# Sixteen projection blocks of a second layer as eight pairs of seven block products, with the shift taken from PSUM and the values centred in their turn

## The chip, the cores and the metric

The kernel runs on one core of one Trainium2 chip. Its time is the device time of the execution in microseconds; the time of a kernel is the median of its runs. Before the change the median of 3 runs is 2240.72 us (2239.9 to 2247.26).

## What is computed

A two-layer model over 1024 tokens of width 1024, in float32. The first layer (a state-space mixer, stick-breaking attention and a feed-forward block) isn't touched. The second is a hybrid layer: one projection `u = h @ w_in` of the normalised input feeds a gated linear attention (GLA) of 4 heads and an RWKV-7 recurrence of 8 heads. Cut to what matters here:

```python
h = _rmsnorm(x, norm_w)
u = (h @ w_in).astype(f32)
gla_u, rwkv_u = u[..., :GLA_IN], u[..., GLA_IN:]
gq, gk, gv, glr, gg = _split(gla_u, GLA_SPLITS)
log_a = jax.nn.log_sigmoid(glr @ gla_gate_up + gla_gate_bias) / GLA_TAU
o = _gla_chunked(q, k, v, log_a)              # chunks of 64 tokens
gla_out = rms(o) * gla_norm_w * jax.nn.silu(gg)
prev = jnp.pad(shifted_cols, ((0, 0), (1, 0), (0, 0)))[:, :-1]
mixed = shifted_cols + (prev - shifted_cols) * rwkv_mu
r, rk, rv, wl, al = _split(mixed, RWKV_SHIFT_SPLITS)
y = _rwkv7_scan(r_h, decay, k_h, v_h, kk, a)  # y linear in v
mu = jnp.mean(y, axis=-1, keepdims=True)
var = jnp.mean(jnp.square(y - mu), axis=-1, keepdims=True)
y = (y - mu) * lax.rsqrt(var + RWKV_GN_EPS) * rwkv_ln_w + rwkv_ln_b
rwkv_out = (y + bonus) * jax.nn.silu(rg)
return x + jnp.concatenate([gla_out, rwkv_out], axis=-1) @ w_out
```

## The kernel before

Five engines have a queue of instructions each, written out by hand in one block per phase; they meet at semaphores. The change lies in two phases.

**`second_in_phase`** (L2847) computes the projection in 30 blocks of 128 output columns: block 0 (the two low-rank parts), 1 to 12 (keys, receptances and values of four RWKV head pairs), 13 (narrow: the GLA gate's 16 columns), 14 to 25 (GLA queries, keys, values and gates) and 26 to 29 (RWKV gates). A block's weights are 128 partitions x 1024 float32, two raw buffers deep. SP loads them; POOL scales them by `WSCALE` (L2981); ACT makes the float16 high part (L3215); POOL subtracts it for the low part (L2987); PE multiplies high x high, high x low and low x high over 8 slices of the contraction and 2 halves of the tokens, 48 matmuls of 512 columns (`product`, L3022 to L3024); ACT empties PSUM (L3235). The input's own parts lie in `second_x_hi` and `second_x_lo` (`S.xhi`, `S.xlo`).

Around the blocks each engine works through the rest, one piece per block. DVE mixes each of blocks 0 to 12 with its shift by one token (L3330 to L3332: a difference, then a multiply-add), makes keys (L3347), receptances (L3358) and values (L3371 to L3382), and then, in this order with solving steps between, the GLA gate (L3430 to L3443), its query and key factors (L3452 on) and the GLA units. POOL computes `keys` (L2995) for each head pair. The solving steps (`substitute`, L3410 to L3424) invert a triangular system for all chunks at once, loaded by SP as one transfer (L2963) of what was parked in DRAM; step n needs step n - 1. The eight GLA units of 128 tokens (0 to 7) start at block 22: PE's turns (L3110), scores (L3116), states (L3124), outputs (L3133 to L3136) and sums (L3151) lie before (`amid`) and after (`behind`) the products, and use DVE's `unit_front` (L3460), `unit_squares` (L3468) and `unit_state` (L3476) and ACT's `unit_out` (L3271) and `unit_sums_out` (L3276). All of a unit waits for the state of the unit before it.

The first layer's `ffn_up_phase` (L2076 on) already multiplies pairs of blocks by seven block products. There SP loads (L2160), POOL forms the sums of the weights (L2197 to L2202), DVE makes the low parts (of the weights L2459, of the next input L2474) and ACT the high parts (of that input L2363). `LAST_USE` (L2073) names the product that reads a part last.

**`rwkv_units_phase`** (L3490) runs the recurrence in eight units of 128 tokens. Per unit PE transposes the parked vectors (`turned`, L3673), makes the maps (L3692 to L3712) and `recur`, then `means` (L3773) and `variances` (L3777) of the unit before; ACT copies the removal factors (L4001), key-values (L4005) and y (L4021) out of PSUM, squares (L3981) and takes roots (L3986, L3988); DVE subtracts the mean (`deviation`, L3879), forms `result` (L3887 to L3893) and `gated` (L3897, L3899). The order of each queue is the order of its loop over c, from -1 to 7. ACT's and DVE's loops before open as:

```python
for c in range(-1, NUNIT):                      # ACT
    if c >= 2:
        high(c - 2)
    if 2 <= c < 2 + GLA_HEADS:
        act.wait_ge(s_gv, 2 * (c - 1))
        nc.scalar.activation(mhi[:, c - 2, :], ...)
    if ahead:
        act.wait_ge(s_akm, n + 1)
        nc.scalar.activation(aa[...], aa_ps, ACT.Copy)   # L4001
```

The output products (L3820 to L3822) end the kernel.

## Time and profile before

| | before |
|---|---|
| median of 3 runs | 2240.72 us |
| runs | 2239.9, 2240.72, 2247.26 us |
| the profiled execution | 2238.72 us |
| its span, first to last instruction | 2237.0 us |
| mean granted clock of TensorE | 0.989 |
| PE busy | 2140.8 us (96%) |
| PE's weight loads (PEld) | 1435.5 us (64%) |
| DVE busy | 1573.6 us (70%) |
| ACT busy | 1001.5 us (45%) |
| POOL busy | 616.3 us (28%) |

The profile is one execution. Busy time is that of instructions which do work; waiting at a semaphore and issuing a DMA don't count. The clock is the share of full speed that TensorE was granted. A "releaser" is what ended an idle time, inferred from the semaphores. PE is matrix work, DVE VectorE, ACT ScalarE, POOL GpSimd, and SPq the queue of the engine that issues the loads. Names are those of buffers in the program: `wraw_z`, `whi_z`, `wlo_z` are the raw weights and their two parts, `ps` is PSUM, and the working arrays (`second_work`, `ffn_out`, `z`, `down_squares`) carry different things in different phases.

### The profile page before, as it was taken

How to read it: one execution, taken by the hardware profiler on the slowest of the kernel's cores; microseconds unless marked ns; L12 is line 12 of the kernel's file. 1: busy time of each engine (PE TensorE's matmuls, PEld its weight loads, DVE VectorE, ACT ScalarE, POOL GpSimd, SP SyncE). 2: the span in 40 equal slices, each digit the busy share in tenths (PEclk: the TensorE clock that was granted, in tenths of full speed). 3: DMA queues.
4: the chain of work that ended last, by engine and by line, in shares of the span. 5: the costliest groups of instructions: out<-in, count | busy, mean ns of one | idle time of the engine just before them, and what ended most of it. 6: DMA issues, size and time to landing. Idle time of an engine off the chain costs nothing. (4 is left out here: it accounts for less than half of the span.)

```text
span 2237.0 us, 45699 instructions
## 1 busy us (share of the span) xinstructions
PE 2140.8 (96%) x19060; PEld 1435.5 (64%) x19060; DVE 1573.6 (70%) x2081; ACT 1001.5 (45%) x1772; POOL 616.3 (28%) x399
## 2 busy tenths in 40 slices
PE   7999999999999899899999999999999999989998
PEld 4666665656666566568888885458644445578757
DVE  6966888988888655887888884256687675246654
ACT  3227775666666443544444443245554332124321
POOL 4456763200001220043333321000155432101160
PEclk9999999999999999999999999999999999999999
DMA  3113213677777622211111115326333622033422
GB/s 138 48 41 112 84 59 88 128 145 145 142 142 142 142 99 73 100 57 53 58 58 58 58 44 189 100 77 215 122 109 108 179 95 86 10 99 100 169 62 76
DMA packets 292086, 224.25 MB, mean 100 GB/s; under 512 B 205537, under 2 KB 255905, under 8 KB 290481
## 3 DMA queue, kind: packets, MB, share of 16 engines
q1 hardware_dynamic: 291888, 221.44, 36.1%
q8 instruction: 146, 2.39, 0.4%
q14 instruction: 52, 0.42, 0.1%
HBM read 148.46 MB, written 28.86 MB: 79 GB/s over the span
## 5 line engine op out<-in xcount | busy, mean ns | idle before, releaser
L1543 DVE TENSOR_TENSOR_SCAN att_left<-att_left,att_unseen_prefix 16x16 f32<-16x16 f32 (+5 forms) x144 | 183.3, 1274 | 34.2 <-ACT att_left L1382 34.2
L3022 PE MATMUL ps<-second_x_hi,whi_z 128*128 128x512 f16 (+1 forms) x480 | 178.8, 372 | 3.4 <-POOL wlo_z L2987 1.9
L1276 PE MATMUL ps<-x_hi,whi_z 128*128 128x348 f16 x560 | 176.0, 314 | 3.4 <-DVE att_q L1487 3.4
L3024 PE MATMUL ps<-second_x_hi,wlo_z 128*128 128x512 f16 (+1 forms) x480 | 178.5, 372 | 0.0
L3023 PE MATMUL ps<-second_x_lo,whi_z 128*128 128x512 f16 (+1 forms) x480 | 178.5, 372 | 0.0
L1278 PE MATMUL ps<-x_hi,wlo_z 128*128 128x348 f16 x560 | 174.9, 312 | 0.0
L1277 PE MATMUL ps<-x_lo,whi_z 128*128 128x348 f16 x560 | 174.8, 312 | 0.0
L2987 POOL TENSOR_TENSOR wlo_z<-wraw_z,whi_z 128x1024 f16<-128x1024 f32 x28 | 65.7, 2348 | 177.9 <-ACT whi_z L3215 177.9
L1502 DVE SCALAR_TENSOR_TENSOR att_left_split<-att_left,att_left_split 128x256 f16<-128x256 f32 (+7 forms) x128 | 106.9, 835 | 7.2 <-ACT att_left_split L1396 7.2
L1396 ACT ACTIVATE att_left_split<-att_left 128x256 f16<-128x256 f32 (+7 forms) x128 | 86.7, 679 | 38.1 <-DMA att_left_turned<-att_left_split 28.6
L1382 ACT ACTIVATE att_left<-ps 16x16 f32<-16x16 f32 (+5 forms) x144 | 86.1, 598 | 37.7 <-PE ps L1292 37.4
L3215 ACT ACTIVATE whi_z<-wraw_z 128x1024 f16<-128x1024 f32 x28 | 29.6, 1056 | 132.4 <-PE ps L3024 117.3
L1323 PE MATMUL ps<-att_left_turned,att_v_tokens 128*64 128x128 f16 x1728 | 63.3, 226 | 25.6 <-DMA att_left_turned<-att_left_split 18.3
L3022 PEld LDWEIGHTS ps<-second_x_hi,whi_z 128*128 128x128 f16 x480 | 46.9, 98 | 62.4 <-issue 6.3
L1234 POOL CAST att_v_meta_split<-att_v_meta 32x128 f16<-32x128 f32 x8 | 9.5, 1183 | 275.4 <-ACT att_v_meta L1388 275.4
L1276 PEld LDWEIGHTS ps<-x_hi,whi_z 128*128 128x128 f16 x560 | 54.7, 98 | 42.2 <-issue 14.7
L1323 PEld LDWEIGHTS ps<-att_left_turned,att_v_tokens 128*64 128x64 f16 x1728 | 53.2, 114 | 44.2 <-issue 34.8
L3023 PEld LDWEIGHTS ps<-second_x_lo,whi_z 128*128 128x128 f16 x480 | 47.0, 98 | 53.5 <-issue 3.6
L3024 PEld LDWEIGHTS ps<-second_x_hi,wlo_z 128*128 128x128 f16 x480 | 46.9, 98 | 53.3
L219 PE MATMUL ps<-x_hi,whi_xbc 128*128 128x348 f16 x240 | 75.6, 315 | 4.6 <-DVE x_lo L529 4.6
L2246 PE MATMUL ps<-x_hi,whi_z 128*128 128x257 f16 (+1 forms) x288 | 78.5, 273 | 0.0
L2247 PE MATMUL ps<-x_lo,whi_z 128*128 128x257 f16 (+1 forms) x288 | 78.4, 272 | 0.0
(694 smaller groups left out, 6675.6 us busy)
## 6 DMA issues: line engine op xcount, KB each, us to landing
wraw_z<-in_w_second SPq DMA_DIRECT2D x30, 512.0 KB, 3.7
wraw_z<-in_w_up SPq DMA_DIRECT2D x26, 512.0 KB, 3.6
wraw_z<-in_w_qkv SPq DMA_DIRECT2D x24, 512.0 KB, 4.7
wraw_z<-in_w_down SPq DMA_DIRECT2D x20, 512.0 KB, 3.8
raw_down<-in_w_down SPq DMA_DIRECT2D x20, 512.0 KB, 4.1
seg<-dt_a_sums SPq DMA_DIRECT2D x18, 512.0 KB, 5.0
...
```

The costliest lines, as they stand in the source:

```text
L1276: nc.tensor.matmul(lin_ps(g), hi, xhi, start=(kb == 0), stop=False)
L1277: nc.tensor.matmul(lin_ps(g), hi, xlo, start=False, stop=False)
L1278: last = nc.tensor.matmul(lin_ps(g), lo, xhi, start=False, stop=(kb == DB - 1))
L1323: nc.tensor.matmul(o_ps(n)[half(a)], vt[:, t.p % 2, (NSTEP - 1) * (x + 1) - t.j + m, half(a)], turned[t.slot][:, keys_at(t, a) + y * t.j + ...
L1382: nc.scalar.activation(of_head(t, a, 0, t.wide), z_ps(a)[0:t.rows, 0:t.wide], ACT.Sigmoid, scale=-0.125).then_inc(s_keep, 1)
L1396: last = nc.scalar.activation(left_part(e, 0, P * t.j), of_head(t, a, 0, P * t.j), ACT.Copy, scale=PSCALE)
L1502: last = nc.vector.scalar_tensor_tensor(low_, of_head(t, a, 0, P * t.j), PSCALE, high, ALU.mult, ALU.subtract)
L1543: nc.vector.tensor_tensor_scan(x, x, unseen, 1.0, ALU.mult, ALU.max).then_inc(s_scan, 1)
L2246: nc.tensor.matmul(out, hi, xhi, start=first and j == 0, stop=False, skip_group_check=True)
L3022: nc.tensor.matmul(out, hi, xhi, start=(j == 0), stop=False)
L3023: nc.tensor.matmul(out, hi, xlo, start=False, stop=False)
L3024: return nc.tensor.matmul(out, lo, xhi, start=False, stop=(j == DB - 1))
```

## The change

1. Blocks 14 to 29 are computed as 8 pairs. A pair's weights are the 2 x 2 blocks A11, A12 (first block, two halves of the contraction), A21, A22, and four sums S1 = A21 + A22, S2 = S1 - A11, S3 = A11 - A21, S4 = A12 - S2; the input has four sums of quarters likewise (`t16`). Seven products (P1 to P7) of 12 matmuls of 512 columns each take the place of 96. They stand on PE in the order P1, P4 of the pair before, P2, P6, P5, P7, P3. Two halves are added up inside PSUM; ACT copies P1, U2 (P1 + P6) and P5 out (`keep`), and DVE adds three of the four results (`quarter`) from PSUM.
2. POOL scales nothing any more and makes no low parts: the scale is folded into ACT's high part and DVE's low part. POOL forms the sums of the weights (`combine`), in which S1 and S2 lie in a buffer of their own and S3 and S4 in place of A11.
3. The sums and parts of the input are made in the first 12 blocks (`t_sums`, `t_lows` on DVE, `t_highs` on ACT).
4. The mix reads the shifted block from PSUM: ACT empties with a scale per column, and DVE adds in one operation. Both scales are small tables made at the start.
5. Gate, keys, solving steps and GLA units stand at new places in the pairs (`SOLVED_AT`; `gate_keys` in pair 3 ahead of A22's low part). SP's waits for A11, U (A21 and A22) and A12 are new.
6. In the RWKV units the values are turned by a product with `center` (identity less the mean of 64) in place of the transpose, so that y comes out centred. `means` and `deviation` go, `variances` take the place of `means`, DVE's `gated` moves to ahead of `keys`, and ACT's `high` and the gated part move behind the copies of the removal.

The diff, cut to its core, with the common indentation left out:

```diff
+SEVEN0 = GLA0 + 1
+SEVENS = (SECOND_B - SEVEN0) // 2
+ORDER_2 = ("P1", "P2", "P6", "P5", "P7", "P3", "P4")
+SPLITS_2 = ("A11", "A12", "S2", "S1", "S3", "S4", "A22")
+FIRST_GATED = (GLA0 + GG - SEVEN0) // 2
+FIRST_G = (G0 - SEVEN0) // 2
+T2_ROUNDS = DB // 2
+SOLVED_AT = {2: (1, 8), 3: (8, 14), 4: (14, 20), 5: (20, 26), "first gate": (26, HALF - 1)}
...
+        t16 = [ctx.enter_context(nc.sbuf_tensor(n, [P, 4, DB // 2, BANK], F16)) for n in ("t2_hi", "t2_lo")]
+        kept = ctx.enter_context(nc.sbuf_tensor("seven_kept", [P, 3, BANK], F32))
+        mu_prev, mu_now = (kept[:, 2, a * 16:a * 16 + GLA0] for a in range(2))
...
-    for i in range(SLOTS, SECOND_B):
...
+    for i in range(SEVENS):
+        g, u = L.w[SEVEN0 + 2 * i], L.w[SEVEN0 + 2 * i + 1]
+        if i == 0:
+            sp.wait_ge(L.cut, SEVEN0 - 1)
+        else:
+            sp.wait_ge(s_slo, split_low(i - 1, "S3"))
+        sp.dma_start(s32["A11"], half(g, 0)).then_inc(s_in["A11"], 16)
+        if i == 0:
+            sp.dma_start(s32["A12"], half(g, 1)).then_inc(s_in["A12"], 16)
+            sp.wait_ge(L.cut, SEVEN0)
+        else:
+            sp.wait_ge(s_comb, combined(i - 1, 4))
+            sp.wait_ge(s_slo, split_low(i - 1, "A22"))
+        sp.dma_start(L.raw[:, 1, :], u).then_inc(s_in["U"], 16)
+        if i:
+            sp.dma_start(s32["A12"], half(g, 1)).then_inc(s_in["A12"], 16)
+        if i < 2:
+            park(2 + i)
+            park_a(2 + i)
+        if i == 1:
             sp.wait_ge(s_asb, RWKV_P * 4 * 16)
             sp.wait_ge(s_parked[RWKV_P - 1], PARKS * 16)
+            sp.wait_ge(s_solve, 1)
...
-    def scaled(i):
-        if i < SECOND_B:
-            pool.wait_ge(L.landed[i % SLOTS], 16 * (i // SLOTS + 1))
-            raw = L.raw[:, i % SLOTS, :]
-            nc.gpsimd.tensor_scalar(raw, raw, WSCALE, 1.0, ALU.mult, ALU.mult).then_inc(s_w64, 1)
-
-    def low_part(i):
...
-            nc.gpsimd.tensor_tensor(L.lo[:, w, :], L.raw[:, w, :], L.hi[:, w, :], ALU.subtract).then_inc(L.cut, 1)
...
+    def combine(i):
+        pool.wait_ge(s_in["U"], in_(i, "U"))
+        pool.wait_ge(s_in["A11"], in_(i, "A11"))
+        if i:
+            pool.wait_ge(s_slo, split_low(i - 1, "S1"))
+        else:
+            pool.wait_ge(C.added, DB)
+        nc.gpsimd.tensor_tensor(s32["S1"], s32["A21"], s32["A22"], ALU.add).then_inc(s_comb, 1)
+        pool.wait_ge(s_comb, combined(i, 1))
+        nc.gpsimd.tensor_tensor(s32["S2"], s32["S1"], s32["A11"], ALU.subtract).then_inc(s_comb, 1)
+        pool.wait_ge(s_comb, combined(i, 2))
+        pool.wait_ge(s_slo, split_low(i, "A11"))
+        nc.gpsimd.tensor_tensor(s32["S3"], s32["A11"], s32["A21"], ALU.subtract).then_inc(s_comb, 1)
+        pool.wait_ge(s_in["A12"], in_(i, "A12"))
+        pool.wait_ge(s_slo, split_low(i, "A12"))
+        nc.gpsimd.tensor_tensor(s32["S4"], s32["A12"], s32["S2"], ALU.subtract).then_inc(s_comb, 1)
+
+    for b in range(RWKV_P - 1):
+        keys(b)
+    combine(0)
+    keys(RWKV_P - 1)
+    pool.wait_ge(s_tlo, t_split(T2_ROUNDS - 1))
+    nc.gpsimd.memset(flat[:, SUB * SUB:2 * SUB * SUB], 0.0).then_inc(s_solve, 1)
+    for i in range(1, SEVENS):
+        combine(i)
...
+    def block_product(i, name, out, of, start, end):
+        pe.wait_ge(s_slo, split_low(i, name))
+        for j in range(DB // 2):
+            hi, lo = (part16(i, name, part)[:, j * P:(j + 1) * P] for part in range(2))
+            xhi, xlo = of(j)
+            nc.tensor.matmul(out, hi, xhi, start=start and j == 0, stop=False, skip_group_check=True)
+            nc.tensor.matmul(out, hi, xlo, start=False, stop=False, skip_group_check=True)
+            last = nc.tensor.matmul(out, lo, xhi, start=False, stop=end and j == DB // 2 - 1, skip_group_check=True)
+        last.then_inc(s_p, 1)
...
+    def seven(i):
+        j = SEVEN0 + 2 * i
+        if i == 0:
+            pe.wait_ge(s_mixed, GLA0 - 1)
+        elif i >= 2:
+            pe.wait_ge(s_c21, nth_c21(i - 2))
+        block_product(i, "A11", bank_a(i), x_of(0, 0), True, False)
+        if i:
+            behind(j - 1)
+            fourth(i - 1)
+        pe.wait_ge(s_quarter, nth_quarter(i - 1, "C11") if i else GLA0)
+        block_product(i, "A12", bank_b, x_of(0, DB // 2), True, True)
+        amid(j)
+        if i == 0:
+            pe.wait_ge(s_tlo, t_split(T2_ROUNDS - 1))
+        pe.wait_ge(s_kept, nth_kept(i, "P1"))
+        block_product(i, "S2", bank_a(i), t_of(2), False, False)
+        if i == 0:
+            removal(RWKV_P - 1)
+        if i:
+            pe.wait_ge(s_quarter, nth_quarter(i - 1, "C12"))
+        block_product(i, "S1", bank_c, t_of(1), True, False)
+        behind(j)
+        pe.wait_ge(s_kept, nth_kept(i, "U2"))
+        block_product(i, "S3", bank_a(i), t_of(3), False, False)
+        if i == 0:
+            gate_products()
+        if i < SEVENS - 1:
+            amid(j + 1)
+        pe.wait_ge(s_kept, nth_kept(i, "P5"))
+        block_product(i, "S4", bank_c, x_of(1, DB // 2), False, True)
...
+    for i in range(SEVENS):
+        seven(i)
+    amid(SECOND_B - 1)
+    fourth(SEVENS - 1)
+    behind(SECOND_B - 1)
+    amid(SECOND_B)
+    behind(SECOND_B)
...
+    empty(GLA0)
+    for name in SPLITS_2[2:]:
+        part_high(0, name)
+    for i in range(SEVENS):
+        c = 2 * i - (UNIT0 - SEVEN0)
+        if i:
+            part_high(i, "S4")
+        act.wait_ge(s_p, made(i, "P1"))
+        if i:
+            act.wait_ge(s_quarter, nth_quarter(i - 1, "C11"))
+        keep(p1, bank_a(i))
+        if i:
+            if there(c - 2):
+                unit_sums_out(c - 2)
+            if i - 1 == FIRST_GATED:
+                nc.scalar.preload_act_table(ACT.Silu)
+            fourth_out(i - 1)
+            part_high(i, "A22")
+        part_high(i + 1, "A11")
+        if i - 1 >= FIRST_GATED:
+            gated(i - 1)
+        if i == 1:
             act.wait_ge(s_gv, 2)
             nc.scalar.activation(low, low, ACT.Exp).then_inc(s_exps, 1)
             act.wait_ge(s_exps, 1)
             nc.scalar.activation(low, low, ACT.Ln, bias=1.0).then_inc(s_ga, 1)
-        if j == GLA0 + 5:
+        if i == 2:
             act.wait_ge(s_gv, 5)
             nc.scalar.activation(low, gb, ACT.Exp).then_inc(s_ga, 1)
             nc.scalar.activation(gx, gb, ACT.Exp, scale=-1.0).then_inc(s_ga, 1)
-        if j == GLA0 + 6:
+        if there(c - 1):
+            unit_out(c - 1)
+        part_high(i + 1, "A12")
+        act.wait_ge(s_p, made(i, "P6"))
+        if i:
+            act.wait_ge(s_quarter, nth_quarter(i - 1, "C12"))
+        keep(u2, bank_a(i))
+        part_high(i + 1, "S2")
+        act.wait_ge(s_p, made(i, "P5"))
+        if i:
+            act.wait_ge(s_quarter, nth_quarter(i - 1, "C22"))
+        keep(p5, bank_c)
+        if there(c - 1):
+            unit_sums_out(c - 1)
+        part_high(i + 1, "S1")
+        if i == 2:
             act.wait_ge(s_gv, 7)
             nc.scalar.activation(low, low, ACT.Exp).then_inc(s_ga, 1)
+        part_high(i + 1, "S3")
         if there(c):
-            unit_sums_out(c)
+            unit_out(c)
...
-        nc.vector.tensor_scalar(d[:, 0:1], ub_[:, 0:1], -1.0, None, ALU.mult)
-        step(nc.vector.tensor_tensor(d[:, 1:SEQ], ub_[:, 0:SEQ - 1], ub_[:, 1:SEQ], ALU.subtract))
-        nc.vector.scalar_tensor_tensor(ub_, d, mu, ub_, ALU.mult, ALU.add).then_inc(s_mixed, 1)
+        nc.vector.scalar_tensor_tensor(now, before, mu_prev[:, mu_at(i):mu_at(i) + 1], now, ALU.mult, ALU.add).then_inc(s_mixed, 1)
...
+    for name in SPLITS_2[2:4]:
+        part_low(0, name)
+    for i in range(SEVENS):
+        c = 2 * i - (UNIT0 - SEVEN0)
+        if i:
+            part_low(i, "S4")
+            if there(c - 1):
+                unit_state(c - 1)
+            if i == 3:
+                gate_keys()
+            part_low(i, "A22")
+            part_low(i + 1, "A11")
+        if i == FIRST_G:
+            substitute(*SOLVED_AT["first gate"])
+        dve.wait_ge(s_p, made(i, "P2"))
+        dve.wait_ge(s_kept, nth_kept(i, "P1"))
+        if i < 2:
+            dve.wait_ge(s_parked[2 + i], PARKS * 16)
+        quarter(c11(i), bank_b, p1)
+        if i == 0:
+            for name in SPLITS_2[4:]:
+                part_low(0, name)
+            part_low(i + 1, "A11")
+            removal_out(RWKV_P - 1)
+        if i == 1:
+            gate_logs()
+            gate_sums(0)
+        if i == 2:
+            gate_query()
         if there(c):
             unit_front(c)
+        part_low(i + 1, "A12")
         if there(c - 1):
             unit_squares(c - 1)
-        if c in rest:
-            substitute(*rest[c])
+        part_low(i + 1, "S2")
         if there(c):
             unit_state(c)
+        dve.wait_ge(s_p, made(i, "P7"))
+        dve.wait_ge(s_kept, nth_kept(i, "P5"))
+        quarter(c22(i), bank_a(i), p5)
+        if i == 0:
+            gate_inputs()
+        if i == 1:
+            gate(gate_sums(1))
+        part_low(i + 1, "S1")
+        if there(c + 1):
+            unit_front(c + 1)
+        dve.wait_ge(s_p, made(i, "P3"))
+        dve.wait_ge(s_kept, nth_kept(i, "U2"))
+        quarter(c12(i), bank_c, u2)
+        if there(c):
+            unit_squares(c)
+        part_low(i + 1, "S3")
+        if i in SOLVED_AT:
+            substitute(*SOLVED_AT[i])
...
+    def turned_centered(c, b, kind):
+        for p in range(RWKV_P):
+            last = nc.tensor.matmul(bank(b)[:, p * P:(p + 1) * P], held(c)[:, kind, p, :], center[:, :], start=True, stop=True)
+        return last
...
-    def means(c):
-        pe.wait_ge(s_y, c + 1)
-        pe.wait_ge(s_rrc, min(c + 2, NUNIT))
-        nc.tensor.matmul(rr_ps, S.same[:, :], y[:, c % 2, :, :].rearrange("p q n -> p (q n)"), start=True, stop=True).then_inc(s_mean, 1)
-
     def variances(c):
         pe.wait_ge(s_sq, c + 1)
+        pe.wait_ge(s_rrc, min(c + 2, NUNIT))
...
-            means(c - 1)
+            variances(c - 1)
...
-        if c >= 1:
-            variances(c - 1)
...
-    def deviation(c):
-        dve.wait_ge(s_mean, c + 1)
-        yc = y[:, c % 2, :, :]
-        nc.vector.scalar_tensor_tensor(yc, rr_ps.rearrange("p (q n) -> p q n", q=RWKV_P), -1.0 / HD, yc, ALU.mult, ALU.add).then_inc(s_dev, 1)
...
+    nc.vector.scalar_tensor_tensor(center[:, :], S.same[:, :], -1.0 / HD, S.ident[:, :], ALU.mult, ALU.add).then_inc(s_center, 1)
...
-        if c >= 1:
-            deviation(c - 1)
+        if 2 <= c < 2 + GLA_HEADS:
+            gated(c - 2)
...
-        if 1 <= c <= GLA_HEADS:
-            gated(c - 1)
...
-        if c >= 2:
-            high(c - 2)
-        if 2 <= c < 2 + GLA_HEADS:
-            act.wait_ge(s_gv, 2 * (c - 1))
-            nc.scalar.activation(mhi[:, c - 2, :], o[:, c - 2, :], ACT.Copy).then_inc(s_ghi, 1)
...
+        if c >= 2:
+            high(c - 2)
...
+        if 2 <= c < 2 + GLA_HEADS:
+            act.wait_ge(s_gv, 2 * (c - 1))
+            nc.scalar.activation(mhi[:, c - 2, :], o[:, c - 2, :], ACT.Copy).then_inc(s_ghi, 1)
```

## Rows read from the trace of the kernel before

**Rows 1.** Windows: stretch, us, busy (count) of PE, PEld, DVE, ACT, POOL, PEclk, DMA.

```profile
1612.00:1758.60 146.60, 143.79 (x845) 64.92 (x843) 118.55 (x84) 68.75 (x67) 81.19 (x36) 1.00 0.39 119
1758.60:1974.20 215.60, 210.75 (x1420) 106.58 (x1416) 103.74 (x142) 50.74 (x54) 59.39 (x32) 1.00 0.25 80
```

**Rows 2.** PE's waits from 1758.6, then from 1974.2: total us, times, longest.

```profile
PE ps L3151 <- DVE down_squares L3468: 1.4, 1, 1.4
...
PE ps L3133 <- ACT ffn_out L3276: 0.8, 1, 0.8
...
PE ps L3673 <- ACT ru_removal L4001: 4.2, 5, 1.6
```

**Rows 3.** Windows, columns as in rows 1, two slices running.

```profile
1813.00:1831.00 18.00, 18.00 (x85) 8.21 (x84) 17.22 (x23) 9.23 (x7) 7.42 (x4) 1.00 0.10 36
1831.00:1849.10 18.10, 18.10 (x86) 8.16 (x85) 17.32 (x19) 2.41 (x3) 6.73 (x4) 1.00 0.18 58
```

**Rows 4.** Timeline of PE: start, us, engine, line, operation, out<-in, [idle before, releaser].

```profile
1954.93 0.38 PE L3022 MATMUL ps<-second_x_hi,whi_z 128*128 128x512 f16 x1
...
1957.95 0.38 PE L3024 MATMUL ps<-second_x_hi,wlo_z 128*128 128x512 f16 x1
```

**Rows 5.** Timelines of DVE, POOL and SP's queue, a pair of the first layer.

```profile
1084.13 1.74 DVE L2474 TENSOR_TENSOR second_x_lo<-gate_conv,second_x_hi 128x512 f16<-128x512 f32 x1 [0.22 <-ACT second_x_hi L2363]
...
1089.78 0.67 DVE L2459 SCALAR_TENSOR_TENSOR s_lo<-down_squares,s_hi 128x512 f16<-128x512 f32 x1
1090.38 0.68 DVE L2459 SCALAR_TENSOR_TENSOR s_lo<-wraw_z,s_hi 128x512 f16<-128x512 f32 x1
...
1084.05 1.27 POOL L2202 TENSOR_TENSOR wraw_z<-wraw_z 128x512 f32<-128x512 f32 x1 [2.76 <-DVE wlo_z L2459]
...
1092.60 0.33 SPq L2160 DMA_DIRECT2D wraw_z<-in_w_up  x1
...
1096.27 1.27 POOL L2197 TENSOR_TENSOR down_squares<-wraw_z 128x512 f32<-128x512 f32 x1 [7.29 <-DMA wraw_z<-in_w_up]
```

**Rows 6.** DVE's timeline through solving, gate and keys.

```profile
1812.67 1.88 DVE L3410 TENSOR_SCALAR z<-z 128x2048 f32<-128x2048 f32 x1
...
1818.46 2.29 DVE L3443 SCALAR_TENSOR_TENSOR second_work<-second_work,ffn_out 128x2048 f32<-128x2048 f32 x1
...
1825.99 0.47 DVE L3415 TENSOR_TENSOR second_work<-z 128x300 f32<-128x300 f32 x1
...
1839.81 0.70 DVE L3452 MEMSET ffn_out<- 128x768 f32 x1 [0.23 <-DVE z L3418]
...
1846.80 0.66 DVE L3415 TENSOR_TENSOR second_work<-z 128x480 f32<-128x480 f32 x1
```

**Rows 7.** Timelines of PE, DVE and POOL around the last values and keys.

```profile
1754.15 1.88 PE L3085 MATMUL ps<-ffn_out,same_chunk 128*128 128x512 f32 x4
...
1760.87 1.22 DVE L3372 TENSOR_TENSOR second_work<-second_work,ffn_out 128x1024 f32<-128x1024 f32 x1
...
1764.44 2.35 POOL L2995 TENSOR_TENSOR z<-second_work,ffn_out 128x1024 f32<-128x1024 f32 x1 [4.77 <-DVE second_work L3375]
```

**Rows 8.** SP's timeline; DMA issues: name, count, KB each, median us to landing.

```profile
1790.54 0.33 SPq L2963 DMA_DIRECT2D z<-removals  x1
...
z<-removals SPq DMA_DIRECT2D x1, 2048.0 KB, 7.7
```

**Rows 9.** PE's timeline in the first layer, and a window as in rows 1.

```profile
50.65 0.47 PE L219 MATMUL ps<-x_hi,whi_xbc 128*128 128x348 f16 x1 [3.58 <-DVE x_lo L529]
...
54.00:56.00 2.00, 2.00 (x8) 1.06 (x7) 1.97 (x3) 0.00 (x0) 0.00 (x0) 0.50 0.00 0
```

**Rows 10.** PE's timeline in one RWKV unit: means, transposes, products.

```profile
2057.08 1.12 PE L3773 MATMUL ps<-wraw_z,same_chunk 128*128 128x512 f32 x2
2058.04 1.04 PE L3673 MATMUL ps<-ident,second_work 128*128 128x128 f32 x8
...
2045.25 2.05 PE L3712 MATMUL ps<-down_squares,ffn_out 128*128 128x128 f32 x16
```

More of the change, by code:

```diff
@@ new lines, in second_in_phase @@
+        s32 = {"A11": half(L.raw[:, 0, :], 0), "A12": half(L.raw[:, 0, :], 1), "A21": half(L.raw[:, 1, :], 0), "A22": half(L.raw[:, 1, :], 1),
+               "S1": half(both, 0), "S2": half(both, 1), "S3": half(L.raw[:, 0, :], 0), "S4": half(L.raw[:, 0, :], 1)}
+        w16 = [{"A11": half(w[:, 0, :], 0), "A12": half(w[:, 0, :], 1), "A22": half(w[:, 1, :], 1),
+                "S1": x[:, 0, BANK:], "S2": x[:, 1, BANK:], "S3": x[:, 2, BANK:], "S4": x[:, 3, BANK:]} for w, x in ((L.hi, S.xhi), (L.lo, S.xlo))]
@@ L2892, in second_in_phase @@
+        first16 = {name: [half(kept[:, n, :].bitcast(F16), part) for part in range(2)] for n, name in enumerate(("A11", "A12"))}
+        part16 = lambda i, name, part: first16[name][part] if i == 0 and name in first16 else w16[part][name]
+        bank_a = lambda i: S.ps[:, 2 + i % 2, :]
+        bank_b, bank_c = S.ps[:, 0, :], S.ps[:, 1, :]
+        p1, u2, p5 = (kept[:, n, :] for n in range(3))
+        t_temps = [half(flat[:, SUB * SUB:SUB * SUB + 2 * SEQ], n) for n in range(4)]
         s_parked = [sem(f"parked{b}") for b in range(RWKV_P)]
@@ L2921, in second_in_phase @@
         K_, R_, V_ = range(3)
+        c11, c12, c21, c22 = ((lambda i, a=a, n=n: half(place(SEVEN0 + 2 * i + a), n)) for a in range(2) for n in range(2))
+        narrow_ps = S.ps[:, 4:6, :]
         with nc.Block() as block:
```

297 lines of the change are left out of this document (192 added, 105 removed).

## The prediction

> **What bounds the kernel now.** I read the stages first [rows 1]. From 1612.0 to 1758.6 us, the first 14 projection blocks, TensorE (PE) is busy 143.8 of 146.6 us; from 1758.6 to 1974.2, the 16 blocks that become pairs, 210.75 of 215.6. PE is the bound, so a matmul taken away is a gain unless a wait takes its place, and new work that must be ready before a product counts in full. Its longest waits come next [rows 2]: in the second stretch 1.4 and 0.8 us, both behind the last unit, and in the RWKV units 4.2 us on ScalarE (ACT) line 4001. The third view tells who has room, by slices as long as a coming pair [rows 3]: VectorE (DVE) is busy 17.2 of 18.0 and 17.3 of 18.1 us in two slices running; gate, keys and the solving steps lie there. These slices are where I expect trouble, since a pair gives DVE ten more steps.
>
> **Matmuls.** Successive 512-column matmuls start 0.216 us apart: 14 steps in 3.02 us [rows 4]. A pair was 2 x 48 of them and becomes 7 x 12 = 84. Eight pairs save 96 x 0.216 = **-20.7 us**. A block product is 12 x 0.216 = 2.6 us. The first layer already runs such pairs, so the prices of the parts are in the trace [rows 5].
>
> **First 14 blocks.** Each mix had two 1024-wide operations on DVE and gets one; DVE takes the low parts over from GpSimd (POOL), one of that width per block, so these two cancel. The sums and low parts for the pairs, 48 steps of 0.6, are spread over 12 blocks of over 10 us each, and POOL no longer locks DVE out there. I cost this at nothing: it hides behind PE; if it does not, the linear of the next block waits for its low part. PE's idle 146.6 - 143.8 = 2.8 [rows 1] stands before the first squares and low parts, which now come earlier: **-2.5** (0 to -2.8).
>
> **What a pair needs.** In the new queues ACT copies U2 out of PSUM only after it has split A12 of the next pair; that load is issued after U, and U after DVE's low part of this pair's A22. P7, which follows P1, P4 of the pair before, P2, P6 and P5 (5 x 2.6 = 13.0 us), waits for that copy. So each pair has the chain: DVE's queue up to A22, two loads, ACT 0.6 + 0.6. Prices [rows 5]: a 512-wide DVE step 0.60, from start to start; U of 512 KB from issue at 1092.60 to its first reader at 1096.27 = 3.7; A12 right behind it has half the bytes: between 0 (they travel together) and 3.7 (they do not overlap) more, taken as 1.0, near the first, as both are in flight at once. So 4.7 + 1.2 = 5.9 us after A22. Counted from the end of P3 of the pair before:
> - Pair 3: C12 0.6, S3 0.6, the solver's head and steps 1 to 5 5.8 (1812.67 to 1818.46), steps 6 and 7 2.1 (four operations of 0.47 to 0.54), S4 0.7, gate_keys 7.0 (1839.81 to 1846.80) or, if POOL's work beside it took 1.8 of that, 5.2; A22 0.7 [rows 6]. Together 15.7 to 17.5, with 5.9 21.6 to 23.4, against 13.0. PE waits 8.6 to 10.4; I take **9.5**.
> - Pair 0: linear 12 ends at 1754.15 and ACT empties it by 1755.4. DVE then has the mix 1.2, five value steps of 1.14 and six pieces of 0.6 up to A22 [rows 7]: 1766.1, so P7 may start at 1772.0; PE is there at 1758.6 + 10.4 + 1.0 (removal) = 1770.0. That is 2.0. POOL's two key products of 2.35 fall on it and can add 4.7. I take **4.5**.
> - Pair 1: the solver's load of 2 MB is issued as now, at 1790.5, and takes 7.7 us [rows 8]; A11 of pair 2 lies behind it, and ACT does exp, ln (3.8 us) and two splits before the copy: about 1804 against 1798.8 at which PE arrives. **4.5** (1.5 to 7).
> - Pair 2: S3 1.2, load 2.7, split, two exps 3.8, split, copy, and a lag of 2.5 to 5 from the gate's scans: 12 to 15.5 against 13. **2** (0 to 2.5).
> - Pair 4: 1.2 + solving 6.5 + 1.4 + 5.9 = 15.0 against 14.9, as unit 0 lies between; unit 1 may wait for its state. **1.5** (0 to 3.5).
> - Pair 5: PE reaches the turns of unit 2 after 3 products and 1.6 of unit 1, at 9.4; they wait for state 1, behind 0.6 + 0.7 + 0.6 + 8.2 (six steps of 1.37) + 0.7 + 1.2 = 12.0. **3** (2.7 to 4).
> - Pair 6: the same with 7.0 of solving: 1.6, and its last steps before unit 4's front. **3.5** (1.6 to 6).
> - End: the 0.8 and 1.4 stay: **2.2**.
>
> Sum 30.7 (18.6 to 40.6); 215.6 - 210.75 = 4.85 is there now: **+25.9** (+13.7 to +35.8).
>
> **Clock.** In the first layer PE stood still for 3.58 us before 50.65; from 54 to 56 the granted clock was still 0.50, the lower of its two levels (1.2 of 2.4 GHz) [rows 9]. 5.4 us at half speed lose 2.7. The waits of pairs 0, 1 and 3 are that long; the first may come in two pieces. Two times 2.7: **+5.4** (2.7 to 8.1).
>
> **Units.** The means go: from 2057.08 to 2058.04 is 0.96, eight times = -7.7. The values are turned by a product with a centring matrix instead of a transpose: 8 transposes 1.04, 8 products of that shape 2.05 [rows 10], so 0.13 more each; 32 times = +4.0. DVE's gated pair of steps moves from before the next unit's front to where DVE now waits for the means and computes the deviation, so it is hidden there, and the 4.2 us on line 4001 [rows 2], where the front was late, shrink to about 0.5: -3.7. With the means, the last wait for y ahead of the output products goes, about 1.2 (0 to 2). Together **-8.6** (-6 to -10). If the cover fails, the removal of the next unit waits for the keys.
>
> Sum: -20.7 - 2.5 + 25.9 + 5.4 - 8.6 = -0.5. The profiled execution took 2238.7 (span 2237.0), 2.0 below the median of the runs shown. 2238.7 - 0.5 + 2.0 = **2240**, for the median.
>
> **Rivals.** A measurement of this kernel can tell 0.3%, 6.7 us, from no change.
> - *Forecast, within 0.3%, 0.38*: the seven-product saving is spent on waits behind ACT's copy of U2 and on a clock drop or two.
> - *Waits short, 0.25*: the low ends hold, the waits come to under 24 and the clock drops once; at the most -20.7 + 13.7 + 2.7 - 2.8 - 10 = -17.1: 2224 to 2234. For it: in five of the eight pairs the chain is within 3 us of PE. Against it: pair 3's chain has hardly a low end.
> - *Count of matmuls alone, 0.05*: no new wait, -20.7 - 2.5 - 8.6 = -31.8: 2209. For it: DVE's load rises by only 10 x 0.6 = 6 us a pair, and most slices have that room. Against it: two have not [rows 3], and the chain is one of order, not of load.
> - *Slower, 0.32*: DVE and POOL keep each other out. At 1084.13 a DVE step, 0.68 elsewhere, took 1.74, having started 0.08 after a POOL sum of 1.27 [rows 5]. Each pair has four such sums (5.1 us) and pair 0 the keys; in the pairs where DVE leads, the queue up to A22 grows by up to 4 us. It decides when the waits exceed 38 us; at the top -20.7 + 35.8 + 8.1 - 6 = +17.2: 2247 to 2258. Against it: S1 and S2 are summed while DVE waits for them anyway. The Trainium skill (SBUF — State Buffer, section "SBUF: two separate sides") says that whichever of such two instructions starts first holds the shared ports for its whole length and the other is fully blocked; by that rule the waits lie at their upper ends. The trace agrees for the step at 1084.13: its excess of 1.06 is nearly the whole rest of the POOL sum.
>
> The range for 8 in 10 is 2227 to 2257: it leaves out the matmul count alone and the ends of the two outer cases. Faster 0.30, same 0.38, slower 0.32.
>
> **What would show it.** 84 matmuls a pair at 0.216; PE waiting for ACT's copy ahead of P7, longest in pair 3 (8 to 11 us) and 2 to 7 in pairs 0 and 1; waits of 1.5 to 4 for DVE's state in pairs 5 and 6; a clock of 0.5 for some 5 us behind the longest; the pairs' stretch some 10 us longer than its 215.6, the units some 8 us shorter, without the wait on ACT's removal copy. If PE waits less than 3 us ahead of P7 in pair 3, the main term is wrong, and the time well under 2234.

## The result

Over 16 runs of each the changed kernel takes 2255.09 us (median), the kernel before 2240.09 us. The ratio is 1.0065, 95% interval [1.0055, 1.0076]: **slower by some 15 us**, where no change was forecast. The time lies in the stated range, near its upper end. Two of the 16 executions took 2243.7 and 2246.0 us, at a mean clock of 0.987 and 0.988; the others were at 0.977 to 0.981. The profiled execution took 2256.34 us, its span is 2254.6. The ratio is that of fast runs: two of the 16 runs of the kernel before, of 3156 and 4623 us, are far off the rest and hardly move the median.

First the busy times of the page, then three windows of the changed kernel (columns as in rows 1): the pairs, the RWKV units up to the first output product, and the rest.

```profile
PE 2131.7 (95%) x18980; PEld 1432.6 (64%) x18980; DVE 1635.7 (73%) x2190; ACT 1033.1 (46%) x1852; POOL 555.2 (25%) x375
```

```profile
1758.80:1998.20 239.40, 206.90 (x1324) 103.17 (x1320) 150.85 (x219) 74.57 (x117) 54.77 (x33) 0.91 0.23 73
...
1999.10:2154.80 155.70, 150.54 (x3502) 133.72 (x3502) 98.52 (x161) 56.59 (x79) 20.93 (x16) 0.97 0.40 126
2154.80:2254.60 99.80, 86.88 (x589) 57.42 (x584) 49.28 (x88) 18.28 (x36) 32.56 (x23) 0.97 0.22 75
```

Against the second line of [rows 1] the pairs take 239.4 us, not 215.6: +23.8. The matmuls went as said (1420 - 1324 = 96 fewer), yet PE is busy only 3.9 us less, with a mean granted clock of 0.91 and not 1.00; and it stands still 32.5 us, not 4.85. Of the same two later stretches of the kernel before, these are the windows:

```profile
1975.20:2139.50 164.30, 154.89 (x3486) 131.91 (x3487) 99.50 (x168) 58.52 (x80) 24.39 (x18) 0.98 0.38 123
2139.50:2237.00 97.50, 86.58 (x585) 57.49 (x583) 46.96 (x88) 17.76 (x35) 29.43 (x21) 0.97 0.21 71
```

The units gained 8.6 us and the end lost 2.3.

PE's waits in the pairs of the changed kernel (in total, times, longest):

```profile
PE ps L3260 <- ACT seven_kept L3384: 18.8, 5, 11.0
PE ps L3187 <- DVE ffn_out L3724: 5.8, 3, 2.6
PE ps L3260 <- DVE second_x_lo L3616: 3.6, 1, 3.6
PE ps L3228 <- DVE down_squares L3716: 2.8, 2, 1.4
PE ps L3210 <- ACT ffn_out L3441: 0.8, 1, 0.8
```

L3260 is the first matmul of a block product, L3384 ACT's copies (`keep`), L3616 the low parts, L3187 the turns of a unit, which wait for the state (L3724), L3228 and L3210 its sums and outputs. The longest one is that of pair 3. The chain behind it, by the timelines of DVE, SP's queue, ACT and PE:

```profile
1841.87 0.51 DVE L3662 TENSOR_TENSOR z<-z,second_work 128x336 f32<-128x336 f32 x1
1842.41 0.69 DVE L3616 SCALAR_TENSOR_TENSOR second_x_lo<-wraw_z,second_x_hi 128x512 f16<-128x512 f32 x1
1843.21 0.70 DVE L3701 MEMSET ffn_out<- 128x768 f32 x1
1843.83 2.23 DVE L3702 TENSOR_TENSOR ffn_out<-second_work,ffn_out 128x2048 f32<-128x2048 f32 x1
1846.09 2.29 DVE L3703 TENSOR_TENSOR second_work<-second_work,ffn_out 128x2048 f32<-128x2048 f32 x1
1848.41 1.29 DVE L3616 SCALAR_TENSOR_TENSOR wlo_z<-wraw_z,whi_z 128x512 f16<-128x512 f32 x2
...
1849.55 0.43 SPq L3026 DMA_DIRECT2D wraw_z<-in_w_second  x1
...
1853.54 0.63 ACT L3381 ACTIVATE whi_z<-wraw_z 128x512 f16<-128x512 f32 x1 [15.04 <-DMA wraw_z<-in_w_second]
1854.07 0.58 ACT L3384 ACTIVATE seven_kept<-ps 128x512 f32<-128x512 f32 x1
...
1854.71 0.61 PE L3260 MATMUL ps<-t_hi,second_x_hi 128*128 128x512 f16 x1 [11.00 <-ACT seven_kept L3384]
```

Solving steps, S4's low part, the keys, A22's low part, the load of A12, its high part, and only then the copy of U2 that P7 needs. It is the chain of the forecast, link by link. A list of waits does not show what the last line does with its 0.61: the same matmul takes 0.38 at full clock [rows 4]. The windows around the waits (stretch, us, PE busy, granted clock, DMA):

```profile
1766.00:1772.00 6.00, 4.07 (x12) 0.72 0.00 0
1776.00:1788.00 12.00, 8.13 (x20) 0.72 1.10 331
1843.00:1854.70 11.70, 0.71 (x4) 0.66 0.22 67
1854.70:1862.00 7.30, 7.29 (x21) 0.61 0.00 0
1876.00:1893.00 17.00, 14.03 (x103) 0.80 0.05 19
1901.00:1916.00 15.00, 12.31 (x75) 0.66 0.16 52
...
1884.80:1890.80 6.00, 5.94 (x48) 0.50 0.00 0
1904.80:1914.80 10.00, 9.93 (x65) 0.50 0.24 79
```

Five drops to half clock: two in pair 0, behind waits of 3.64 and 3.87 us, one behind pair 3's wait of 11.0, and one each in pairs 4 and 5, behind waits of only 1.17 and 1.75, and of 2.62 us, the last two of these between a unit's small products. The last two lines are those two drops alone: 0.50 for 6 and for 10 us.

### The profile page after: what moved, and what is told of

It is laid out like the page before. It is cut to its first block and busy times, and to the rows that moved or that the text cites. A ratio compares the mean times of both kernels' runs of the same rounds, so it can differ in the third digit from the quotient of the medians.

```text
span 2254.6 us, 45884 instructions
## 1 busy us (share of the span) xinstructions
PE 2131.7 (95%) x18980; PEld 1432.6 (64%) x18980; DVE 1635.7 (73%) x2190; ACT 1033.1 (46%) x1852; POOL 555.2 (25%) x375
## 5 line engine op out<-in xcount | busy, mean ns | idle before, releaser
L3096 PE MATMUL ps<-second_x_hi,whi_z 128*128 128x512 f16 (+1 forms) x224 | 81.6, 364 | 2.8 <-DVE second_x_lo L1758 1.4
L3097 PE MATMUL ps<-second_x_lo,whi_z 128*128 128x512 f16 (+1 forms) x224 | 81.5, 364 | 0.0
L3098 PE MATMUL ps<-second_x_hi,wlo_z 128*128 128x512 f16 (+1 forms) x224 | 81.5, 364 | 0.0
L2248 PE MATMUL ps<-x_hi,wlo_z 128*128 128x257 f16 (+1 forms) x288 | 78.3, 272 | 0.0
L221 PE MATMUL ps<-x_hi,wlo_xbc 128*128 128x348 f16 x240 | 75.5, 314 | 0.0
L220 PE MATMUL ps<-x_lo,whi_xbc 128*128 128x348 f16 x240 | 75.4, 314 | 0.0
L1278 PEld LDWEIGHTS ps<-x_hi,wlo_z 128*128 128x128 f16 x560 | 54.4, 97 | 28.8
L1277 PEld LDWEIGHTS ps<-x_lo,whi_z 128*128 128x128 f16 x560 | 54.8, 98 | 25.0 <-issue 0.2
```

The costliest lines, as they stand in the source:

```text
L1277: nc.tensor.matmul(lin_ps(g), hi, xlo, start=False, stop=False)
L1278: last = nc.tensor.matmul(lin_ps(g), lo, xhi, start=False, stop=(kb == DB - 1))
L3096: nc.tensor.matmul(out, hi, xhi, start=(j == 0), stop=False)
L3097: nc.tensor.matmul(out, hi, xlo, start=False, stop=False)
L3098: return nc.tensor.matmul(out, lo, xhi, start=False, stop=(j == DB - 1))
```

## The experiments

Each ratio is against runs of the kernel before on the same chip, with its 95% interval. "The stretch" is that from the last values' product to the first product of the RWKV units: 221.1 us before, 244.8 in the changed kernel. Stretches, waits and drops are read from the one profiled execution of each run.

**e1: one copy ahead of the load** (changed kernel, ACT's queue).

```diff
-                    part_high(i + 1, "A12")
                     act.wait_ge(s_p, made(i, "P6"))
                     ...
                     keep(u2, bank_a(i))
+                    part_high(i + 1, "A12")
```

> Only ACT's copy of U2 moves ahead of its high part of A12 of the next pair. Theory (the load stands in a chain of order): the waits ahead of P7, 18.8 us in five pairs of the changed kernel (11.0 in pair 3), go, since the copy then waits for nothing but P6. A12 is wanted 10.4 us later, at P2 of the next pair; in pair 3 this comes out about even, and 1 to 3 us may stay there. The clock drops behind pair 0's second wait and pair 3's go too, some 3 us each. Together 20 to 24 us off 2255: 2231 to 2236. Rival (DVE's work is the limit and any order gives the same): the wait of pair 3 moves to P2 or P6 of pair 4 nearly whole, and the time stays above 2247.

2251.66 us, 1.0051 [1.0033, 1.0069]: the theory missed. The time is the rival's, the place is neither's: P7 of pair 3 waits no longer, but P3 of the same pair waits 10.2 us, and the clock drops six times in the pairs. ACT's timeline there:

```profile
1850.36 0.63 ACT L3381 ACTIVATE whi_z<-wraw_z 128x512 f16<-128x512 f32 x1 [11.10 <-DMA wraw_z<-in_w_second]
1852.86 0.63 ACT L3381 ACTIVATE second_x_hi<-z 128x512 f16<-128x512 f32 x1 [1.88 <-POOL z L3073]
1853.40 0.58 ACT L3384 ACTIVATE seven_kept<-ps 128x512 f32<-128x512 f32 x1
```

The last line is the copy of P5, which P3 waits for. It stands behind A12's high part, which started only with its load (ACT had stood idle for 11.10 us), and behind S2's, which waited 1.88 for POOL's sum. The wait for a load in the middle of this queue holds all that follows it, not the next instruction alone.

**e2: the keys later** (DVE's queue of pair 3).

```diff
-                        if i == 3:
-                            gate_keys()
                         part_low(i, "A22")
                         part_low(i + 1, "A11")
+                        if i == 3:
+                            gate_keys()
```

> Only gate_keys moves, from ahead of the low part of A22 in pair 3 to behind those of A22 and the next A11. Theory: the wait of 11.0 us in pair 3 shrinks by what the keys take of DVE, 5.2, to 5.8 us; its clock drop stays. All else as it was: 2250. Rival (the wait is the load's own length, or the sums on POOL): the wait stays above 9 us, the time at 2255.

2243.52 us, 1.0014 [1.0004, 1.0023]. The wait is 5.30 us, near the 5.8 worked out. The time fell by more, some 11 us in place of 5, and nothing tried here says why: the stretch is 236.8, with 6.1 us less idle and 1.9 less busy time than in the changed kernel, and the profiled execution reached it 2.8 us earlier, in code that is the same in both. Three of its five drops stand behind waits of 1.75, 2.62 and 1.42 us in front of a unit's turns; waits of 1.42 and 1.43 us at that place left the clock whole in the changed kernel, e6, e8 and e12.

**e3: the solving steps later**, behind the state and the low parts of A22 and A11.

```diff
-                    if i in SOLVED_AT:
-                        substitute(*SOLVED_AT[i])
...
+                    if i - 1 in SOLVED_AT:
+                        substitute(*SOLVED_AT[i - 1])
```

> The solving steps move from the end of a pair to behind the unit's state and the low parts of A22 and A11 in the next. Theory: the wait of pair 3 loses the 7.2 us of steps 1 to 7, the three waits of the units' turns for the state (5.8 us) go, and with them two clock drops of about 3 us; the front of a unit is later and may cost up to 3 us in pairs 5 and 6: 2237 to 2243. Rival (DVE is the limit there): the waits move to the unit's fronts and the time stays within 4 us of 2255.

2260.56 us, 1.0094 [1.0077, 1.0112]: the rival held, and worse. Pair 3 waits 3.8 us and the states are in time, but the units' fronts (`unit_front` on DVE, L3708), for which PE's scores wait, are not:

```profile
PE ps L3201 <- DVE ffn_out L3708: 17.0, 3, 7.4
PE ps L3260 <- ACT seven_kept L3384: 10.5, 4, 4.0
```

**e4: these three together.**

> The three moves of the runs beside it together. Theory: of 31.8 us of waits in the pairs about 8 stay (pair 0's first 3.6, the end's 2.2 and some fronts), and one or two of the five clock drops: 2219 to 2227, under the kernel before. Rival (the load of DVE): no better than the best of the three alone, 2235 or more.

2261.78 us, 1.0100 [1.0082, 1.0118]: the rival held. 16.9 us stand in front of L3201, as in e3, 8.2 us in front of copies, and there is a new wait of 2.7 us for C22. DVE comes to C22 late there because 10 us of solving steps now stand ahead of it; by its timeline it waits for no load on the way. That C22, too, has a load's reader ahead of it in DVE's queue is what e8 mends.

**e5 and e6: one part of the change each.** e5 is the kernel before with the new RWKV units, e6 the change without them.

> The kernel before with the change of the RWKV units alone. Theory: what the changed kernel shows between the first product of the units and the end, -6.3 us, holds here too: 2233 to 2236. Rival (the gain hangs on the pairs ahead): within 2 us of the kernel before.

> The change without that of the units. Theory: it costs what the units gain, so 2255 + 6.3 = 2261 (2258 to 2264), and the pairs' stretch is some 24 us longer than the 16 blocks were. Rival (the two parts interact): below 2256.

e5: 2233.79 us, 0.9976 [0.9961, 0.9992]. e6: 2262.14 us, 1.0101 [1.0066, 1.0137]. Both as expected: the units gain 5 to 7 us, the pairs cost some 23, and e6's stretch is 245.9 us.

**e7 and e11: waits put in on purpose** between the large products of the kernel before (e7 as here with copies of 16 columns; e11 with a list of its own and copies of 512).

```diff
+STALLS = {3: 1, 5: 3, 7: 5, 9: 8, 11: 12, 15: 18, 20: 30}
...
+                        if i - 1 in STALLS:
+                            pe.wait_ge(s_out, i)
...
+                    if j - 1 in STALLS:
+                        act.wait_ge(s_lin, j)
+                        for k in range(STALLS[j - 1]):
+                            nc.scalar.activation(...)
```

> The kernel before, with TensorE made to wait on purpose between two blocks at seven places, behind blocks 3, 5, 7, 9, 11, 15 and 20, for about 1.5, 2, 2.5, 3, 4, 5 and 7 us (ACT does small copies before it empties the block; the output is the same). It measures a clock drop by itself. Theory (a wait costs itself, and from some length on a drop of 3 us more): waits as short as those of the pairs without a drop (1.1 to 1.6 us) leave the clock at 1.00, those of 3.6 us and more bring it to 0.50 for about 5 us of work, 2.7 to 3.3 us lost each. With some 25 us of waits and 3 or 4 drops 2274 to 2280. Rival (the drops of the changed kernel have another cause, such as its kind of matmuls): no clock below 1.00 behind any of the seven, 2263 to 2267.

2252.34 us, 1.0054 [1.0033, 1.0075], outside both ranges, since the waits came out shorter than meant (five of 0.5 to 1.2 us, no drop; one of 5.3, one drop of 1.5 us). So once more:

> The kernel before with longer waits put in on purpose, now behind blocks 16, 19, 17, 20 and 18, where nothing else lies between the blocks: about 1.9, 2.5, 3.1, 3.7 and 4.3 us (and two of unknown length behind blocks 7 and 10). The first run of this kind had waits of 0.6 to 1.2 us, without a drop, and one of 5.3 us, with one that cost 1.6 us of work. Theory: waits up to some 2.5 us leave the clock at 1.00, those of 3.7 and 4.3 us bring it to 0.50 and cost 1.5 to 3 us more each. Some 20 us of waits and 2 or 3 drops: 2261 to 2270. Rival (only waits of 5 us and more drop it, those of the pairs dropped for another reason): no drop behind the five.

2278.89 us, 1.0174 [1.0157, 1.0191], over the expected time, as the waits were longer than meant (30.2 us in seven). PE's timeline behind four of them, and the windows behind the last three of these:

```profile
1814.26 0.39 PE L3024 MATMUL ps<-second_x_hi,whi_z 128*128 128x512 f16 x1 [2.78 <-ACT second_work L3239]
1828.90 0.39 PE L3024 MATMUL ps<-second_x_hi,whi_z 128*128 128x512 f16 x1 [4.11 <-ACT second_work L3239]
1846.55 0.61 PE L3024 MATMUL ps<-second_x_hi,whi_z 128*128 128x512 f16 x1 [5.43 <-ACT second_work L3239]
1862.42 0.39 PE L3024 MATMUL ps<-second_x_hi,whi_z 128*128 128x512 f16 x1 [3.45 <-ACT second_work L3239]
```

```profile
1829.00:1835.00 6.00, 6.00 (x21) 0.72 0.29 87
1846.00:1852.00 6.00, 5.45 (x17) 0.63 0.22 82
1862.00:1868.00 6.00, 5.58 (x26) 1.00 0.29 90
```

2.78 and 3.45 us: no drop. 4.11 and 5.43 (and 5.50, 4.17 and 4.77, elsewhere): one each, here of 6.00 x 0.28 = 1.7 and 5.45 x 0.37 = 2.0 us lost. So on the drops the theory held and the rival fell: a wait alone, with the matmuls of the kernel before, is enough. The five drops cost 1.6 to 2.0 us each, less than the 2.7 of the forecast. The 30.2 us of waits and 8.9 of drops give 39 of the 41 us by which the profiled execution is longer.

**e8: both copies first.** On the changed kernel ACT copies U2 and P5 before the high parts of A12 and S2, and DVE adds C22 before their low parts; the exponentials of pairs 1 and 2 stand ahead of A11's high part.

```diff
                     keep(u2, bank_a(i))
-                    part_high(i + 1, "S2")
...
                     keep(p5, bank_c)
+                    part_high(i + 1, "A12")
+                    part_high(i + 1, "S2")
...
                     quarter(c22(i), bank_a(i), p5)
+                    part_low(i + 1, "A12")
+                    part_low(i + 1, "S2")
```

> No work is moved but the loads' readers: ACT copies U2 and P5 before it makes the high parts of A12 and S2 of the next pair (and makes A11's after the exponentials in pairs 1 and 2), and DVE adds C22 before the low parts of A12 and S2. gate_keys and the solving steps stay where the change put them. Theory (the waits ahead of P7 and P3 come from the load in the queue, and the run that moved one copy alone failed because the copy of P5, and C22 on DVE, still stood behind the load): the five waits of 18.8 us go but for about 1 us, and with them two clock drops of 3 us; pair 0's first wait of 3.6 and the units' 5.8 stay. 2228 to 2238. Rival (DVE's load of 5 us of keys and 7 of solving in pair 3 is too much wherever the copies stand): pair 3 still waits over 6 us, somewhere in the five products behind, and the time stays above 2242.

2242.80 us, 1.0018 [1.0007, 1.0030]: above the theory's range and just inside the rival's (over 2242). The waits for copies fell from 18.8 to 0.9 us and the stretch to 230.0, but behind pair 3's solving and keys 3.3 us came up for A12's low part and 3.0 for C21, together the 6 us that the rival had named, and 2.8 for a front. So both hold in part: some 10 to 12 us of the loss are the order of these few instructions, and the rest is not mended by it.

**e9: e8, the keys later, pair 0's low parts of S2 and S1 earlier, solving steps moved.**

The solving steps' part of the edit:

```diff
-SOLVED_AT = {2: (1, 8), 3: (8, 14), 4: (14, 20), 5: (20, 26), "first gate": (26, HALF - 1)}
+SOLVED_AT = {1: (1, 3), 2: (3, 9), 3: (9, 13), 4: (15, 19), 5: (21, 25), "first gate": (25, HALF - 1)}
+SOLVED_LATE = {4: (13, 15), 5: (19, 21)}
```

> As the run with both copies first, and in addition the low parts of S2 and S1 of pair 0 stand ahead of DVE's last two value steps, the keys stand behind the low parts of A22 and A11, two solving steps are made in pair 1, and four in pairs 4 and 5 behind the state and not ahead of it. Theory: pair 0's first wait of 3.6 and most of the units' 5.8 go, with up to three clock drops: 2212 to 2225. Rival (the units' fronts have no room): waits of 2 to 4 us take their place in pairs 4 and 5 as in the run with all solving steps behind, 2230 or more.

2232.30 us, 0.9970 [0.9956, 0.9984]: faster than both kernels, but in the rival's range and not the theory's. The stretch is 222.0; PE waits 4.6 us in front of the last removal product, for POOL's keys, and 4.7 and 1.9 us for a unit's front, as the rival had said.

**e10: four more moves** (the removal product behind P7, the gate products behind P3, gate_logs ahead of A11's low part in pair 1, solving steps spread anew), **and e13: A11's high part behind the copies in pair 0 as well.**

> The run with everything (2232.3) and four more moves: the last removal product stands behind P7 of pair 0 and not ahead of P5 (it had waited 4.6 us for POOL's keys), the gate products behind P3; gate_logs and the first scan stand ahead of A11's low part in pair 1, where DVE waited 5.3 us for a load; the solving steps lie as (1 to 5), (6 to 10), (11 to 13), (14 to 18), (19 to 24), rest. Theory (each wait left is a matter of order): the waits of 4.6, 2.0 and most of 4.7 us go, with the two clock drops behind them: 2215 to 2224. Rival (DVE has no room left in the pairs): new waits take their place, 2229 or more.

> As the run before it (2227.1), and in pair 0 ACT makes the high part of the next A11 behind the copies of U2 and P5, not ahead of them; it waited there for a load while PE waited 6.1 us for the copy. Theory (order): that wait and the clock drop behind it go, some 7.5 us: 2217 to 2222. Rival (pair 0 is short of DVE, and another wait follows): 2225 or more.

e10: 2227.09 us, 0.9941 [0.9925, 0.9958], between its two ranges; e13: 2227.46 us, 0.9949 [0.9930, 0.9967]. These are the best that compute everything, 11 to 13 us under the kernel before and 28 under the changed one. In e10's profile 6.1 us stood in pair 0; that execution took 2234.7 us, the other three 2225.6 to 2228.2, so it shows more than most of them have. e13 took the wait away, and 2.6 us came up in pair 0 and 4.4 in pair 1, behind the solver's load: the rival's case, and no gain over e10.

**e12 and e14: POOL's sums cut to 64 of 512 columns**, on the changed kernel and on e13. Seven eighths of each weight sum are left out. One of the four lines, the others alike:

```diff
-nc.gpsimd.tensor_tensor(s32["S1"], s32["A21"], s32["A22"], ALU.add)
+nc.gpsimd.tensor_tensor(s32["S1"][:, 0:64], s32["A21"][:, 0:64], s32["A22"][:, 0:64], ALU.add)
```

> The changed kernel with POOL's four sums a pair cut to 64 of their 512 columns (the rest of the sums is left out): POOL's share of each pair goes from 5 to under 1 us, all order stays. It tells the slower rival of the prediction (DVE and POOL keep each other out) from the forecast's chain. Theory (order, the load in the queue): pair 3's wait stays above 9.5 us, the others lose 2 to 4 us together: 2249 to 2254. Rival (the lock): DVE's steps of the queue up to A22 get shorter by up to 4 us in the pairs where DVE leads, pair 3's wait falls under 8 us: 2243 or less.

2238.01 us, 1.0000 [0.9990, 1.0009]: 17 us less than the changed kernel. The theory of order alone missed; the time is the rival's, the lock, and pair 3's wait, 8.1 us, lies at its bound of 8. The stretch, first of the changed kernel, then of this one:

```profile
1754.32:1999.14 244.82, 211.38 (x1372) 105.06 (x1373) 155.47 (x226) 75.99 (x119) 56.16 (x33) 0.91 0.24 78
```

```profile
1748.87:1976.95 228.08, 203.39 (x1373) 101.35 (x1372) 143.59 (x224) 76.14 (x119) 23.25 (x33) 0.94 0.26 85
```

No DVE instruction was touched, and DVE is busy 155.5 - 143.6 = 11.9 us less: that is what POOL's sums cost DVE. PE's idle time fell by 33.4 - 24.7 = 8.7 us, and with three drops in place of five its busy time by 8.0. How much of the 8.7 is DVE's slower steps, and how much that the sums themselves are ready sooner, this run does not separate. Here, too, the trace agrees with the Trainium skill (SBUF — State Buffer, "SBUF: two separate sides"), by which a GpSimd instruction and a VectorE one with two SBUF inputs shut each other out.

> The run beside it with POOL's sums cut to 64 of 512 columns (the rest of the sums is left out). Theory A (the lock costs DVE time in any order, but with the order mended DVE has room, so PE sees little of it): 2 to 4 us faster than the run beside it. Theory B (DVE is near its limit in the pairs and the lock is what is left of the waits): 8 us or more faster.

2221.66 us, 0.9919 [0.9898, 0.9940], 5.8 us under e13, between the two theories. With the order mended, the sums cost about 6 us in place of 17; with four and five runs the two intervals just overlap, so the 6 is rough.

**e15: late states** in the kernel before, by copies ahead of `unit_state`.

```diff
+LATE = {1: 13, 2: 14, 3: 15, 4: 16, 5: 17, 6: 18}
...
+                    for k in range(LATE.get(c, 0)):
+                        gate(nc.vector.tensor_copy(late[:, :, :], ...))
```

> The kernel before, with DVE's state of units 1 to 6 made later on purpose by 13 to 18 copies of 0.55 us or so, so that PE waits in front of the turns of units 2 to 7, by about 0.6, 1.2, 1.8, 2.4, 2.9 and 3.5 us. Its clock was 1.00 there. Theory (among the small products of the units a short wait is enough): the clock falls to 0.50 behind the waits from about 1.4 us on, four times, at some 3.3 us each: 2239 + 12.4 + 13 = 2264 (2259 to 2269). Rival (the length of the wait alone decides, as between large products, where 3.45 us left the clock whole): at most one drop, 2251 to 2255.

2256.78 us, 1.0069 [1.0047, 1.0090], between the two: two drops, where the theory had four and the rival at most one. PE's timeline and the windows behind:

```profile
1885.86 0.52 PE L3112 MATMUL ps<-ident,ffn_out 128*128 128x128 f32 x2 [4.58 <-DVE ffn_out L3480]
1908.95 0.41 PE L3112 MATMUL ps<-ident,ffn_out 128*128 128x128 f32 x2 [2.80 <-DVE ffn_out L3480]
...
1944.53 0.41 PE L3112 MATMUL ps<-ident,ffn_out 128*128 128x128 f32 x2 [1.51 <-DVE ffn_out L3480]
```

```profile
1886.00:1898.00 12.00, 11.93 (x73) 0.57 0.01 2
1909.00:1918.00 9.00, 8.94 (x66) 0.62 0.01 2
1945.00:1955.00 10.00, 9.93 (x96) 1.00 0.01 2
```

Between the units' small products 2.80 us dropped the clock, which 2.78 and 3.45 us did not between large ones. 1.51 and 1.25 us did not here, though 1.42 did in e1 and e2, so there is no sharp length. And a drop costs more: 11.93 x 0.43 = 5.1 and 8.94 x 0.38 = 3.4 us.

## Why the prediction was wrong

| term | forecast | measured |
|---|---|---|
| 96 matmuls | -20.7 | -20.7 |
| start and first 14 blocks | -2.5 | +0.2 |
| PE's waits in the pairs | +25.9 | +27.7 |
| clock (busy time beyond the matmuls) | +5.4 | +16.9 |
| RWKV units and end | -8.6 | -6.3 |
| sum, against the span before | -0.5 | +17.8 |

The spans differ by 17.6, the medians by 15.0. The waits are 32.5 - 4.85. The first row is not measured by itself: it is the 96 matmuls, counted, at their pace, and the clock's row is what PE's busy time is longer than that, 206.9 - (210.75 - 20.7). In windows of 2 us the drops hold 16.0 us of it by busy time x (1 - clock): 1.5, 2.7, 2.8, 3.3 and 5.1 for the five, and 0.6 for one that begins behind the last unit's sums. (The wider windows above give 13.2 for the five, too little, since they mix busy time at half clock with idle time at full.) The tails of the last matmuls ahead of waits, 0.16 each (0.38 less the pace of 0.22), are about 1.3 for the eight waits that the pairs have more than the blocks had.

**The step that failed is the clock**, "two times 2.7": +5.4 in the sum, and +16.9 measured, of which 16.0 are time at half clock. The forecast took the one pair of rows [rows 9] as a measure of length, 3.6 us, for all waits. Five drops came, in place of two. Two are in pair 0, whose wait came in two pieces, each with a drop behind it, and one in pair 3. The other two are in pairs 4 and 5, 8.4 us together, where the forecast had put waits of 1.5 and 3 us and no drop: among the units' small products a wait of 2.8 us is enough (e15), and 1.17 and 1.75 us together were. The trace of before had the warning. Its window from 1975.2 to 2139.5 above has a clock of 0.98, and all of that is at its start, behind two waits of 1.42 and 1.09 us around the last unit's sums, with the clock at 1.00 ahead of them:

```profile
1973.02 1.12 PE L3151 MATMUL ps<-down_squares,ones 128*128 128x512 f32 x2 [1.42 <-DVE down_squares L3468]
1975.24 1.99 PE L3649 MATMUL ps<-second_x_lo 64*64 64x64 f32 x64 [1.09 <-PEq L2923]
...
1973.00:1974.00 1.00, 0.98 (x2) 1.00 0.00 0
1975.20:1981.20 6.00, 5.49 (x87) 0.50 0.14 28
```

The forecast left it aside. The other rows miss the same way, by +2.7, +1.8 and +2.3: with the clock right the time would still have been some 7 us over.

**The waits were right in sum, in part by luck.** By pair, forecast and measured: 0: 4.5 and 3.6 + 3.9; 1: 4.5 and 1.1; 2: 2 and 1.6; 3: 9.5 and 11.0; 4: 1.5 and 1.2 + 1.8; 5: 3 and 2.6; 6: 3.5 and 1.4 + 1.4; end 2.2 and 2.2; together 30.7 and 31.8. Pairs 0 and 1 miss by +3.0 and -3.4, which cancel; the others are in place. Pair 0 has a wait that was not in the list, P6 for the low part of S2: DVE's two low parts there took 3.43 us in place of 1.3, beside POOL's product of keys. That pair 1 has less fits that pair 0 had already put PE back; no run shows it by itself. The upper end of the forecast's waits was summed too low as well: with 2.0 + 4.7 for pair 0 its own entries give 42.3, not 40.6. The sign "the pairs' stretch some 10 us longer" failed with the clock: it is 23.8.

**The slower rival named a true mechanism and a wrong way to the sum.** Its time, 2247 to 2258, holds the result, and POOL's sums do cost 11.9 us of DVE's time, 8.7 us of waits and two clock drops (e12). But the waits never passed the 38 us at which it was to decide: they came to 31.8, and the clock made up the rest. I had counted part of the lock in the waits' upper values and gave it one drop more than the forecast, 8.1 us in all. The two terms belong together: a longer wait can bring a drop with it. I treated them as independent.

**First 14 blocks:** from the first product to the last values' product it is 164.84 us before and 163.67 now: -1.2, not -2.5; that first product came 1.34 us later, ahead of all that the forecast had costed. The cover held otherwise, with 1.7 us of waits.

**Units:** the stretch up to the first output product gave 8.6 us, where 7.4 had been put, with the wait on the removal copy down from 4.2 to 0.7 us. The end gave nothing back: without `means` ahead of them the output products start at once, and now the last unit's `variances` waits 2.0 us inside them for ACT's square, where 1.2 us of gain had been put. e5 shows the part alone at -5.
